# A two-block transformer on one core: ScalarE's order beside window attention, and the routing stretch ahead of the experts

## The reference, cut to what matters

```python
# layer 1 of the first block, after layer_norm ln1
logits = xf @ w_router                       # 256 x 8
top_vals, top_idx = lax.top_k(logits, 2)
gates = softmax(top_vals)
y = (silu(xb @ w1[e]) * (xb @ w3[e])) @ w2[e]   # for each token's two experts
e = sigmoid(h @ ple_gate_w + ple_gate_b) * (p @ ple_w)    # the "embedding" and its gates
h = layer_norm(ALPHA * h + moe + e)

# second block, each layer
aq, ak, av, az, mq, mk, mv, mo, mz, mi, mf = split(xn @ w_in)
att = softmax([q k_window, q k_context, sink]) @ v * silu(az)
mq, mk = silu(dwconv([mq, mk]))              # then the scan
```

## Time and profile before

| | us |
|---|---|
| median of 3 runs | 2115.52 |
| lowest and highest run | 2105.86, 2117.64 |
| the profiled execution | 2113.53 |
| its span in the profile | 2111.4 |
| TensorE busy in it | 2031.0 |

### The profile page before, as it was taken

The page is one execution under the profiler, slowest core; times in us unless marked ns, Lnnn a source line. Parts: engine busy times, 40 slices in busy tenths (PEclk is TensorE's granted clock), DMA queues, the critical chain, the costliest instruction groups (busy, mean ns, idle before and its releaser), DMA issues.

```text
span 2111.4 us, 36621 instructions
## 1 busy us (share of the span) xinstructions
PE 2031.0 (96%) x15746; PEld 1463.7 (69%) x15746; DVE 784.3 (37%) x1780; ACT 409.8 (19%) x970; POOL 5.8 (0%) x12
## 2 busy tenths in 40 slices
PE   8999999999989999999999999999999899999997
PEld 6879999986766666666566666665854568465786
DVE  5837556585341110111111110111335545435554
ACT  1233110113320112000010000000223343223332
POOL 0000000000000000000000000000000000000000
PEclk9999999998999999999999999999999999999999
DMA  9483444445069999999999999999121111122120
GB/s 317 175 284 138 162 160 184 176 180 200 20 247 360 420 419 414 421 420 420 420 408 420 421 420 421 420 420 408 40 100 41 41 60 41 63 102 75 61 81 20
DMA packets 72370, 506.72 MB, mean 240 GB/s; under 512 B 7824, under 2 KB 9872, under 8 KB 11792
## 3 DMA queue, kind: packets, MB, share of 16 engines
q1 hardware_dynamic: 71056, 500.15, 59.2%
q0 software_dynamic: 1152, 4.19, 0.9%
HBM read 503.27 MB, written 1.05 MB: 239 GB/s over the span
## 4 chain that ended last, share of the span: by engine, by line
PE 90%; DMA 5%; ACT 3%; DVE 2%; issue 1%; SPq 0%; DVEq 0%; ACTq 0%
PE ps L454 87%; DMA work<-weights 2%; DMA ring<-weights 2%; PE ps L1192 1%; PE ps L745 1%; ACT work L1817 0%; PE ps L621 0%; DMA xc<-x_t 0%; PE ps L1249 0%; DVE work L2745 0%; PE ps L1293 0%; ACT work L1860 0%; ACT work L1588 0%; ACT work L1851 0%; ACT work L1830 0%
## 5 line engine op out<-in xcount | busy, mean ns | idle before, releaser
L454 PE MATMUL ps<-work 128*32 128x256 f32 (+8 forms) x5560 | 586.0, 385 | 11.2 <-ACT work L1830 2.8
L454 PE MATMUL ps<-work,ring 128*128 128x256 f32 (+2 forms) x2056 | 521.2, 408 | 7.4 <-DVE work L2745 5.0
L454 PEld LDWEIGHTS ps<-work 128*32 128x32 f32 (+3 forms) x5560 | 375.9, 138 | 175.4 <-issue 97.4
L454 PE MATMUL ps<-ring,work 128*32 128x256 f32 (+3 forms) x4824 | 473.0, 414 | 14.4 <-DMA work<-weights 4.2
L454 PEld LDWEIGHTS ps<-work,ring 128*128 128x128 f32 x2056 | 352.6, 191 | 144.3 <-issue 108.5
L454 PEld LDWEIGHTS ps<-ring,work 128*32 128x32 f32 (+1 forms) x4824 | 261.4, 121 | 150.6 <-issue 81.7
L454 PE MATMUL ps<-xc,ring 128*128 128x256 f32 (+1 forms) x1440 | 278.0, 354 | 5.6 <-DMA ring<-weights 3.9
L454 PEld LDWEIGHTS ps<-xc,ring 128*128 128x128 f32 x1440 | 243.4, 193 | 41.8 <-issue 7.5
L2287 DVE TENSOR_TENSOR work<-work,ps 128x256 f32<-128x256 f32 x42 | 17.7, 421 | 420.4 <-ACT work L1661 420.4
L454 PE MATMUL ps<-xc,work 128*128 128x256 f32 (+1 forms) x720 | 138.3, 350 | 0.0
L454 PEld LDWEIGHTS ps<-xc,work 128*128 128x128 f32 x720 | 120.9, 191 | 19.8 <-issue 4.6
(11 more groups left out here) (279 smaller groups left out, 1228.1 us busy)
## 6 DMA issues: line engine op xcount, KB each, us to landing
ring<-weights SPq DMA_DIRECT2D x317, 1024.0 KB, 12.0
work<-weights SPq DMA_DIRECT2D x154, 1024.0 KB, 16.0
work<-rel POOLq DMA_DIRECT2D x8, 512.0 KB, 11.2
con<-consts SPq DMA_DIRECT2D x1, 1368.0 KB, 21.6
xc<-x_t SPq DMA_DIRECT2D x1, 1024.0 KB, 7.6
xc<-ctx_t SPq DMA_DIRECT2D x1, 1024.0 KB, 25.7
out<-work SPq DMA_DIRECT2D x4, 256.0 KB, 2.1
par<-params SPq DMA_DIRECT2D x1, 872.0 KB, 9.0
```

The source lines that it names most:

```text
L454: ins = eng.matmul(o, lhs, rhs, start=start, stop=stop, **kw)
```

## The change

Five things change.

1. In the attention of the second block, ScalarE's `yield` moves from the head of the loop to its end: the body of round n now runs ahead of the copies of tiles that were finished in round n.
2. The 11 slots of the experts' stage are taken in the order 1, 2, ..., 10, 0 (`MOE_RING`). The stage's first two units, the gates, so go to slots 1 and 2, whose last units are the last of `w_ada` and the first of `w_out`; before, the first went to slot 0 behind the embedding's own unit.
3. TensorE makes all logits at once, then turns the tokens (banks 1, 6, 7, 2), then the places, then the second half of the embedding's products. ScalarE copies two of the embedding's tiles, does `gate_exp` and `tokens_copy`, then the other two.
4. The ranks are computed for both halves of the tokens in one set of operations.
5. Experts are sorted by one key, the count less a small multiple of the expert's number, and that sort and `order_out` move from `by_tokens` to the head of VectorE's `places`.

```diff
+MOE_RING = [1, 2, 3, 4, 5, 6, 7, 8, 9, 10, 0]
-            slot = (n - MOE_START) % MOE_SLOTS
+            slot = MOE_RING[(n - MOE_START) % MOE_SLOTS]
...
-                    next(products)
-                assert next(products, "ended") == "ended"
-                release[0], held[0] = held[0], 0
+                turn_tokens()
+                places()
+                for _ in products:
+                    pass
...
-                        b = 2 * t + half
-                        o = fill(("htok", t, half), b, (s["h_turned"], b + 1))
+                        b = (1, 6, 7, 2)[2 * t + half]
+                        o = fill(("htok", t, half), b, (s["h_turned"], 2 * t + half + 1))
...
             def block2_attention(l):
                 items = att_pairs(l)
                 for n in range(att_rounds(l)):
-                    yield
                     if 2 <= n < len(items) + 2:
...
                                 .then_inc(s["att_exp"], 1)
+                    yield
...
-                ple_products(l)
                 if l == 1:
+                    ple_products(l, 0, 2)
                     gate_exp()
                     tokens_copy()
+                    ple_products(l, 2, 4)
                     moe()
...
+                bases = con[:, CN.all("bases")]
+                more, by_place = spread[:, 0], spread[:, 1]
+                link(eng.scalar_tensor_tensor(out=place_key, in0=bases, scalar=-0.5 / (EXPERTS * MOE_UNITS),
+                                              in1=o[:, 16:24], op0=ALU.mult, op1=ALU.add))
...
+                eng.tensor_copy(crowded[:, 0:EXPERTS], by_rank[:, 4]).then_inc(s["order_out"], 1)
                 eng.tensor_tensor(slot_of, in_order, rank_t, ALU.mult).then_inc(s["dve_order"], 1)
```

More of the change, by code:

```diff
@@ L264, in build @@
         place_of, one_hot, over, late_gate = cut(EXPERTS), cut(EXPERTS, EXPERTS), cut(EXPERTS), cut(TT, EXPERTS)
+        place_key = cut(EXPERTS)
         over_any = cut(1)
@@ L1426, in _ @@
                     router_beside_embedding()
-                    turn_tokens()
-                    places()
                     moe()
@@ L1614, in block1_out, with ple_products @@
                         .then_inc(s["mix_biased"], 1)
-            def ple_products(l):
-                for c in range(4):
+            def ple_products(l, first=0, end=4):
+                for c in range(first, end):
                     o = tile(eng, "ple", l, c)
@@ L2157, in routing @@
                     .then_inc(s["gate_exp"], 1)
[L2158 to L2168, removed]
+                before = con[:, CN.all("before")].rearrange("p (a b) -> p a b", b=8).unsqueeze(1)
+                other = logits.unsqueeze(2).broadcast_to([P, TT, 8, 8])
+                own = logits.unsqueeze(3).broadcast_to([P, TT, 8, 8])
+                gc, ge = (v.rearrange("p a (b c) -> p a b c", c=8) for v in (gcmp, geq))
+                eng.tensor_tensor(gc, other, own, ALU.is_gt)
+                link(eng.tensor_tensor(ge, other, own, ALU.is_equal))
+                link(eng.tensor_tensor(ge, ge, before.broadcast_to([P, TT, 8, 8]), ALU.mult))
+                link(eng.tensor_tensor(gc, gc, ge, ALU.add))
+                link(eng.tensor_reduce(rank_t, gc, AX.X, ALU.add))
                 eng.tensor_scalar(rank_t, rank_t, float(TOP_K), None, ALU.is_lt).then_inc(s["chosen_out"], 1)
@@ L2180, in places @@
                 in_order = o[:, 0:16].rearrange("p (a b) -> p a b", b=8)
+                bases = con[:, CN.all("bases")]
+                more, by_place = spread[:, 0], spread[:, 1]
+                link(eng.scalar_tensor_tensor(out=place_key, in0=bases, scalar=-0.5 / (EXPERTS * MOE_UNITS),
+                                              in1=o[:, 16:24], op0=ALU.mult, op1=ALU.add))
+                link(eng.tensor_tensor(more, place_key.unsqueeze(1).broadcast_to([P, 8, 8]),
+                                       place_key.unsqueeze(2).broadcast_to([P, 8, 8]), ALU.is_gt))
+                link(eng.tensor_reduce(place_of, more, AX.X, ALU.add))
+                link(eng.tensor_tensor(one_hot, place_of.unsqueeze(1).broadcast_to([P, 8, 8]),
+                                       con[:, CN("slot", 0, 8)].unsqueeze(2).broadcast_to([P, 8, 8]), ALU.is_equal))
+                link(eng.tensor_tensor(by_place, one_hot, bases.unsqueeze(1).broadcast_to([P, 8, 8]), ALU.mult))
+                link(eng.tensor_reduce(by_rank[:, 4], by_place, AX.X, ALU.add))
+                eng.tensor_copy(crowded[:, 0:EXPERTS], by_rank[:, 4]).then_inc(s["order_out"], 1)
                 eng.tensor_tensor(slot_of, in_order, rank_t, ALU.mult).then_inc(s["dve_order"], 1)
@@ L2188, in by_tokens @@
             def by_tokens():
[L2190 to L2204, removed]
+                for a, b in ((0, 4), (5, 6)):
+                    link(eng.tensor_tensor(spread[:, a:b], one_hot.unsqueeze(1).broadcast_to([P, b - a, 8, 8]),
+                                           by_expert[:, a:b].unsqueeze(2).broadcast_to([P, b - a, 8, 8]), ALU.mult))
+                    link(eng.tensor_reduce(by_rank[:, a:b], spread[:, a:b], AX.X, ALU.add))
             def choose():
```

1 line of the change is left out of this document (added).

## The result

| | us |
|---|---|
| before, median of 4 runs | 2114.72 (2105.86 to 2117.64) |
| after, median of 4 runs | 2078.26 (2075.97 to 2090.35) |
| ratio | 0.983, 95% interval 0.981 to 0.986 |
| the profiled execution after | 2075.97, its span 2073.8 |

A forecast was written before the change was run, and what follows sets the result against it. TensorE, busy 2031.0 of 2111.4 us, was taken as the bound, so only its idle or low-clock time pays. Attention 16.7 plus routing 5.0 gave 21.7 us: profiled 2091.8, median 2093, forecast range 2088 to 2100, whole range 2083 to 2104.

The forecast's parts named there:

- the median on the other side of the clock's choice: First block's layer 1 attention, clock 0.50 from 509 to 529 us, may fall either way: 2084, chance 0.13.
- The attention: Second block's attention: 16.5 us of TensorE waits go, less 1.5 for new waits, plus 1.7 of clock: 16.7 us.
- The 1.5 us held back for new waits: Attention: allowance for new waits in which VectorE comes late, between 0 and 6 us possible, 1.5 taken.
- the clock at 1652: Second block's attention: clock 0.57 between 1652 and 1656 behind a long wait; 1.7 us lost there come back.
- The routing: Routing stretch: gates reached 3.3 us earlier, plus 1.7 us of clock; steps of the experts 5.0 us earlier.
- rival 1: Routing stretch: the clock falls, products and first gates at half clock; 3.7 us less gain, 2097, chance 0.09.
- the gates at full clock: Routing stretch: without the idle gap ahead, the gates take 14.5 us instead of 16.16, a gain of 1.7.
- The stream of loads: Experts' stage: loads start 4.8 us earlier and move with TensorE's steps, so the experts' end moves the whole 5.0.
- Rival 2: Experts' stage: the full stream of loads hides the routing gain; gain 16.7 only, 2099, chance 0.07.
- Rivals 3 and 4: Attention: VectorE's rounds become the bound, 2101 to 2103 (0.09); tile copies held behind late exponentials, 36 us lost, 2129 (0.02).

The follow-up runs named there:

- repeated kernel: The changed kernel run again unaltered, six runs: median 2090.57 us, ratio 0.988 against a before of 2119.23.
- pair with constant matmuls: Changed kernel with unread constant matmuls in both layers of the first block's attention, 2080.02 us, beside the unaltered changed kernel, 2090.57.
- routing parts alone: The changed kernel with ScalarE's attention order put back (items 2 to 5 alone): median 2111.93 us over 12 runs, ratio 0.997 against before.

## Why the prediction failed, step by step

**The clock of the first block: the step that failed.** The forecast is 2113.5 less 21.7 us of gains, with nothing for the first block: I took one fall of 20 us in layer 1 for both sides, and gave "the median on the other side of the clock's choice" 0.13, at 2084. That case came, in three of four runs: 9.5 us by the trace. The repeated kernel and the pair with constant matmuls show that the changed kernel falls as well, so that this part was luck and no effect that can be counted on; in the second set of six the same kernel has a median of 2090.57, inside my range. It was an error of the range and not only bad luck, though. The runs of before had shown the gap of 9.7 us already, with one run of three at its lower side. And I put the case at 2084 with the attention at its likeliest size, and the low end 1 us under it, so that a term that came out 4 us larger was enough to leave the range. The 37.6 us between the spans are my 21.7, 9.5 here, 4.2 in the attention, 2.7 in the two stretches with a short fall of before alone, and -0.5 in the rest.

**The attention: right in its mechanism, mis-sized.** 14.0 + 6.9 = 20.9 us measured, 16.7 forecast; the kernel with this edit alone gives 20.2 in its times. Two things were missing. The 1.5 us held back for new waits did not occur: TensorE's list has none. And the listed idle time understates each wait. Two rows of TensorE before, in a round without a wait:

```profile
1602.82 3.70 PE L454 MATMUL ps<-work,ring 128*128 128x512 f32 x8
1606.36 1.04 PE L1192 MATMUL ps<-con,work 128*128 128x128 f32 x8
```

The piece ends, as modelled, at 1606.52, but the next transposes start at 1606.36. A matmul that is not held up starts 0.16 us ahead of the modelled end of the one before, and the idle time is counted from that end. 16 waits by 0.16 are 2.6 us. So 16.5 + 2.6 + 1.7 for the clock at 1652 = 20.8, against the 20.9 measured. That the difference is made of just these two is worked out, not tested by a run of its own.

**The routing: near in size, made of other parts.** 4.7 us against 5.0. The logits end 4.97 us behind the first of them (forecast 4.79). The places were to come 7.1 us behind it and came 8.21; the gates were to start 3.3 us earlier and start 15.27 - 12.78 = 2.5 us earlier. What lies between is the mechanism of rival 1: the clock fell, to 0.52 and 0.63, and the 16 transposes, which the places have to wait for, took 3.55 us instead of 1.91. It was back before the products and the gates, so by these differences it cost 0.8 to 1.1 us here and not the 3.7 of that rival; the gates at full clock gave 2.2 us where I had 1.7. It was no accident of this execution: the clock fell in this stretch in all six traces of the changed order. In two of them (the changed kernel again, and the routing parts alone) it fell earlier, the logits took 6.1 us, the first step came 41.6 behind the first logits, and the part was worth 3.5 us; the times of the routing parts alone say 3.1. In the old order, with products between the logits, the same 16 transposes ran at full clock in all eight traces. I had given the fall 0.09, and that was too little for something that came each time. The Trainium skill ("TensorE: Matmul & The Clock Gate", Part 4: PE-mode transpose) says that transposes do not count as busy for the clock in the way matmuls do. These traces do not bear it out. After, the clock fell at 580.1 us, as the logits ended and before the transposes had done anything; in the two traces just named it fell within the logits. And it came back to 1.00 at 583.5, when TensorE had run nothing but transposes since 580.2; in all six traces it came back within 0.9 us of their end. What stood ahead of each fall are the small logits matmuls that wait for VectorE's chunks.

**The stream of loads: right.** From the experts' first step to the second block's start it takes 852.27 us before, 851.27 after and 850.9 to 853.5 in the other kernels, whose first steps lie up to 6 us apart relative to the logits. Rival 2 is refuted. The waits for loads in 600 to 1480 us, after; before, the first kind was 7.5 us, with 3.9 of them ahead of the first gate, and the second 5.5:

```profile
PE ps L456 <- DMA ring<-weights: 5.8, 5, 1.4
...
PE ps L456 <- DMA work<-weights: 3.5, 4, 1.3
```

**Rivals 3 and 4** are refuted by the list of waits: no transposes behind VectorE, nothing behind the tile copies.

**In sum:** with the fall out of the way the change is worth 25.8 to 26.5 us, where I had 21.7. The other 10 us of the measured 36 are the luck of the draw.

## What to carry to other kernels

Where two engines feed each other in rounds, look at what the slower consumer does first in its round: ScalarE idled 4 us in front of a tile copy that nobody wanted soon, while work that TensorE needed next lay ready; moving one `yield` was worth 20 us. Before moving many things to hide one wait, try the smallest edit that takes its cause away: the two gate units in free slots took the wait away alone, and three further edits added nothing that a trace or a time shows. And when the single runs of a kernel lie in two groups, tell them apart by the mean clock, compare like with like, and let the range's low end start from the lower group with every term at its largest.

## What was not expected of the hardware

- The same code at the same place ran at 1.00 or at 0.50 from one execution to the next. In the first block's attention a fall lasts 17 to 27 us and costs some 10, and every row that stands wholly at 0.50 shows TensorE busy 2.00 of 2 us; layers 0 and 1 fall each by itself. What decides it in a given execution stays open: the traces of kernels with and without it do not differ in anything that I could name.
- Short falls of 4 us, 1.7 us each, come besides, and some differ between executions of the same code: between the two layers of the second block's attention the first trace of the changed kernel has none, its second trace has two in a row (1796 to 1806 us).
- Eight matmuls on constants took the falls away in the profiles: in 35 runs of four kernels with them no clock under 0.991, where 48 of 58 runs of before were at 0.989 or less. (By the clock alone a short fall in the few at 0.991 can't be excluded.) By the medians they cost 3 to 6 us themselves, so they buy a narrower spread: 3.5 us over twelve runs of before, instead of 14.7.
- Work moved out from between small matmuls can bring the clock down: with the products behind the places the logits took 4.97 us in the first trace instead of 6.73, and the clock fell at their end or within them, in six traces of six. The experts' first step comes 40.4 to 41.6 us behind the first logits in that order. In the old one with the same slots it comes at 38.9 in two traces, and at 40.5 and 40.6 in the two in which the clock fell under the gates.
